# Inverse roots of memory between the forget exits, a warm-up tile written by VectorE, and the weight column on ScalarE's queue

## The reference

```python
def rmsnorm(x, w):
    xf = x.astype(jnp.float32)
    y = xf * lax.rsqrt(jnp.mean(xf * xf, axis=-1, keepdims=True) + EPS)
    return (y * w.astype(jnp.float32)).astype(x.dtype)

def token_mix(h, w_in, ...):
    proj = h @ w_in
    (hq, hf, hi, hgate, gq, gk_, gv, ggate, glr) = jnp.split(proj, idx, axis=-1)
    f = lb + (1.0 - lb) * jax.nn.sigmoid(hf)
    ...
    gdecay = jax.nn.log_sigmoid(glr @ gla_w_gk2 + gla_b_gk) / GLA_GATE_NORMALIZER
    ...

def reference(x, mem, norm_mix_w, w_in, ...):
    h = rmsnorm(x, norm_mix_w)
    x = x + token_mix(h, w_in, ...)
    x = x + cross_attend(rmsnorm(x, norm_xa_w), rmsnorm(mem, norm_mem_w), w_xq, w_xkv, w_xo)
    x = x + moe(rmsnorm(x, norm_moe_w), w_router, b_router, w_gate_up, b_gate_up, w_down, b_down)
    return rmsnorm(x, norm_final_w)
```

## Time and profile before

| | |
|---|---|
| median of three runs | 1184.41 us |
| profiled execution, whole | 1184.76 us |
| span of the profiled execution | 1183.0 us |
| TensorE busy | 1134.4 us (96%) |
| VectorE busy | 381.3 us (32%) |
| ScalarE busy | 181.8 us (15%) |
| read from memory | 442.55 MB |

### The profile page before, as it was taken

One profiled execution on the slowest core, in us unless ns is written; L12 is line 12 of the kernel. 1 busy time (PEld: TensorE's weight loads), 2 busy tenths in 40 slices (PEclk: granted clock), 3 DMA queues, 4 the chain that ended last, 5 costly groups with the idle time before them and its releaser, 6 DMA issues.

```text
span 1183.0 us, 18703 instructions
## 1 busy us (share of the span) xinstructions
PE 1134.4 (96%) x7502; PEld 574.9 (49%) x7503; DVE 381.3 (32%) x891; ACT 181.8 (15%) x395; POOL 22.0 (2%) x65
## 2 busy tenths in 40 slices
PE   9999999999999999999999999999999999999996
PEld 8989889855434444344333333333333333333332
DVE  4988878455221111222211111111111111111112
ACT  4611521343100000000000000000000000000002
POOL 4000010000000000000000000000000000000000
PEclk9999999999999999999999999999999999999999
DMA  9954204989999999999999999999999999999995
GB/s 324 369 172 144 73 10 155 346 330 398 417 428 432 429 431 431 429 433 431 433 430 433 431 430 433 431 431 433 431 433 430 432 432 431 432 432 423 426 424 226
DMA packets 41353, 444.24 MB, mean 376 GB/s; under 512 B 4270, under 2 KB 5656, under 8 KB 24540
## 3 DMA queue, kind: packets, MB, share of 16 engines
q1 hardware_dynamic: 39868, 440.45, 88.9%
q0 software_dynamic: 480, 1.85, 0.6%
q10 hardware_dynamic: 960, 1.31, 0.4%
HBM read 442.55 MB, written 1.05 MB: 375 GB/s over the span
## 4 chain that ended last, share of the span: by engine, by line
PE 67%; DMA 31%; DVE 1%; ACT 0%; SPq 0%; issue 0%; DVEq 0%; ACTq 0%
DMA ring<-in_w_gate_up 30%; PE bank L1180 23%; PE bank L1171 13%; PE bank L736 7%; PE bank L732 4%; PE bank L1210 4%; PE bank L1225 3%; PE bank L875 1%; PE bank L715 1%; PE bank L1107 1%; PE bank L1296 1%; PE bank L1201 1%; PE bank L1287 1%; PE bank L913 1%; PE bank L1019 1%; PE bank L1141 1%
## 5 line engine op out<-in xcount | busy, mean ns | idle before, releaser
L1180 PE MATMUL bank<-ring,region 128*64 128x512 f32 x2048 | 464.0, 608 | 36.0 <-DMA ring<-in_w_gate_up 36.0
L1180 PEld LDWEIGHTS bank<-ring,region 128*64 128x64 f32 x2048 | 147.0, 140 | 333.5 <-issue 268.7
L1171 PE MATMUL bank<-ring,region 128*64 128x512 f32 x1024 | 226.8, 595 | 0.3 <-ACT region L1419 0.3
L2328 DVE TENSOR_SCALAR region<-bank 128x512 f32<-128x512 f32 x32 | 22.1, 691 | 573.9 <-PE bank L1180 573.9
L1171 PEld LDWEIGHTS bank<-ring,region 128*64 128x64 f32 x1024 | 71.1, 137 | 130.1 <-issue 127.2
L1419 ACT ACTIVATE region<-bank 128x256 f32<-128x256 f32 (+1 forms) x130 | 53.4, 437 | 367.0 <-PE bank L1171 251.1
L1419 ACT ACTIVATE bank<-region 128x512 f32<-128x512 f32 x32 | 19.2, 601 | 452.5 <-DVE region L2328 452.5
L736 PE MATMUL bank<-ring 128*128 128x256 f32 x392 | 86.6, 380 | 0.0
L736 PEld LDWEIGHTS bank<-ring 128*128 128x128 f32 x392 | 73.8, 190 | 10.9 <-issue 0.7
L1210 PE MATMUL bank<-region 64*128 64x512 f32 x264 | 65.6, 615 | 0.1
L1225 PEld LDWEIGHTS bank<-region,r_levels 128*128 128x128 bf16 x1536 | 61.3, 118 | 1.6 <-issue 1.6
(11 more groups left out here) (318 smaller groups left out, 774.0 us busy)
## 6 DMA issues: line engine op xcount, KB each, us to landing
ring<-in_w_gate_up SPq DMA_DIRECT2D x48, 4096.0 KB, 30.2
ring<-in_w_down SPq DMA_DIRECT2D x24, 4096.0 KB, 36.5
ring<-in_w_gate_up SPq DMA_DIRECT2D x26, 2048.0 KB, 14.3
ring<-in_w_down SPq DMA_DIRECT2D x10, 2048.0 KB, 13.3
ring<-in_w_in SPq DMA_DIRECT2D x6, 2048.0 KB, 19.8
ring<-in_w_gate_up SPq DMA_DIRECT2D x11, 1024.0 KB, 35.6
ring<-in_w_xkv SPq DMA_DIRECT2D x4, 2048.0 KB, 11.0
ring<-in_w_down SPq DMA_DIRECT2D x7, 1024.0 KB, 8.3
```

What stands on the lines that cost most here:

```text
L1171: last = pe.matmul(bk[half * ROWS:(half + 1) * ROWS, :], lhs, w[:, half * 512:(half + 1) * 512], start=start, stop=stop, skip_group_check= ...
L1180: last = pe.matmul(rows, lhs, columns[:, half], start=start, stop=stop, skip_group_check=True)
L2328: v.tensor_scalar(g_t, bank_g[:, :], LIMIT, None, ALU.min).then_inc(sem["g_clamped"], 1)
```

## The change

Five things are done. The weight column w_mix is issued as the first transfer of ScalarE's queue, ahead of the first part of the forget panel, instead of on SyncE's queue between x's two halves. TensorE's warm-up reads a tile `warm` that VectorE fills with ones as its first instruction, seven products instead of six, and TensorE waits for the identity only after them; an eighth product, on the identity, follows flip_x(0). The loops over token halves and over the first two parts of the forget panel change places: the first half goes through parts 0 and 1 with flip_x(1) between them, then the second half. The mem_sum product stands ahead of m = 3 of the last forget products instead of after them. And VectorE computes the inverse roots of memory between scale_forget(0) and scale_forget(1) instead of between keys_of_forget(0) and keys_of_forget(1).

```diff
-WARM_UP = 6
+WARM_UP = 7
+        warm = r_t[:, 0:P]
@@ sync
             load_x(0)
-            sp.dma_start(w_mix, by_row(A["norm_mix_w"][0])).then_inc(sem["w_mix_in"], 16)
             load_x(1)
@@ tensor
+            def keep_busy(tile, n):
+
+                c = (3 - n // 2) * P
+                pe.matmul(banks[6 + n % 2][:, c:c + P], tile, tile, start=True, stop=True)
+
+            pe.wait_ge(sem["warm_ready"], 1)
+            for n in range(WARM_UP):
+                keep_busy(warm, n)
             pe.wait_ge(sem["ident_ready"], 1)
-            for n in range(WARM_UP):
-                c = (3 - n // 2) * P
-                pe.matmul(banks[6 + n % 2][:, c:c + P], ident[:, :], ident[:, :], start=True, stop=True)
...
             flip_x(0)
+            keep_busy(ident[:, :], WARM_UP)
...
-            for i, (k0, k1) in enumerate(zip(FIRST_ROWS[:2], FIRST_ROWS[1:3])):
-                pe.wait_ge(first_in[i], 16)
-                for t in range(NT):
-                    if (t, k0) == (1, 0):
+            for t in range(NT):
+                for i, (k0, k1) in enumerate(zip(FIRST_ROWS[:2], FIRST_ROWS[1:3])):
+                    if (t, i) == (0, 1):
                         flip_x(1)
+                    pe.wait_ge(first_in[i], 16)
                     for m in range(4):
                         ins = forget(k0, k1, t * P, (t + 1) * P, m)
...
             for m in range(4):
+                if m == 3:
+                    pe.wait_ge(sem["mem_squared"], 1)
+                    end(pe.matmul(begin("mem_sum")[:, 0:8], same_row, mem_sums, start=True, stop=True), "mem_sum")
                 ins = forget(*FIRST_ROWS[2:], 0, T, m)
                 if m % 2 == 1:
                     end(ins, f"hf{m // 2}")
-
-            pe.wait_ge(sem["mem_squared"], 1)
-            end(pe.matmul(begin("mem_sum")[:, 0:8], same_row, mem_sums, start=True, stop=True), "mem_sum")
@@ scalar
+            act.dma_start(w_mix, A["norm_mix_w"][0].rearrange("(p k) -> p k", k=KT)).then_inc(sem["w_mix_in"], 16)
             act.dma_start(panel(0)[:, k, :], first_panel[:, k, :]).then_inc(first_in[0], 16)
@@ vector
+            v.memset(warm, 1.0).then_inc(sem["warm_ready"], 1)
             dve.wait_ge(sem["ident_ready"], 1)
...
             scale_rows(0)
             scale_forget(0)
+            wait_full(dve, "mem_sum")
+            taken(v.tensor_scalar(mem_sums, bank_of("mem_sum")[:, 0:8], EPS, None, ALU.add), "mem_sum")
+            wait_taken(dve, "mem_sum")
+            newton_steps(mem_rstd, mem_sums).then_inc(sem["mem_rms"], 1)
             scale_forget(1)
             scale_rows(1)
...
             keys_of_forget(0)
-            wait_full(dve, "mem_sum")
-            taken(v.tensor_scalar(mem_sums, bank_of("mem_sum")[:, 0:8], EPS, None, ALU.add), "mem_sum")
-            wait_taken(dve, "mem_sum")
-            newton_steps(mem_rstd, mem_sums).then_inc(sem["mem_rms"], 1)
             keys_of_forget(1)
```

More of the change, by code:

```diff
@@ L133 @@
 SEMS = """quarter_joined rows_summed first_product seventh_product first_kept seventh_kept t1_ready t2_ready t3_ready t4_ready w_mix_in pads_zeroed glr_ready hT_scaled mem_in vec_in cols_in glr_in router_in moe_row_in final_row_in down_bias_in gu_bias_in
- consts_ready ident_ready masks_ready s_zeroed x_squared x_diag mem_squared mem_rms mem_scaled mem_turned mem_weighed hf_streamed lb_diff lb_sigmoid lnf_ready
+ consts_ready warm_ready ident_ready masks_ready s_zeroed x_squared x_diag mem_squared mem_rms mem_scaled mem_turned mem_weighed hf_streamed lb_diff lb_sigmoid lnf_ready
  z_abs z_ln scanned first_sigmoids r_diff r_exp r_ready gate_sigmoid gate_ready y_ready x1_squared
```

## The result

| | before | after |
|---|---|---|
| median of 19 runs each, us | 1184.41 | 1186.03 |
| lowest to highest, us | 1183.77 to 1186.52 | 1184.10 to 1189.64 |
| profiled execution, span | 1184.76, 1183.0 | 1186.46, 1184.7 |

The ratio after to before is 1.0015 with a 95% interval of 1.0008 to 1.0022. I had forecast 1183.9 in a range of 1183.0 to 1185.0: "within 0.2%" held, but the sign and the range didn't. The two profiled executions differ by 1.70 us, as the medians do (1.62), so they can be read against each other.

The account below looks back on a forecast made before the run. TensorE's progress up to about 270 us was taken to release the expert weight stream that sets the end. Terms 0 + 0 + 0 - 0.49 gave -0.5 us, so 1183.9 us (chance 0.60), range 1183.0 to 1185.0.

Parts of the forecast that it names:

- within 0.2%: Whole kernel's time: no change beyond 0.2%, which means 2.4 us; chance 0.93, against faster 0.04 and slower 0.03.
- The frame: Whole kernel: a microsecond won on TensorE up to 270 us moves the expert weight stream and the end one for one.
- The query panel as a floor: Queries' start: panel lands at 23.68, so TensorE's earlier savings are spent waiting; products start at 23.70 as now, gain 0.
- Warm-up and forget order: Ahead of the query panel: earlier warm-up gains 0 to 1.5 us, token-half order saves 0.3; both taken as 0.
- Memory's roots: VectorE between the forget exits: moving the inverse roots removes the gap among the gs products, -0.49 us.
- The wait for z: VectorE after the roots' move: next limited by z, ending at 32.94; L1895 starts about 33.05, so 0.57 survives.
- The weight column: Front loads: column lands some 0.4 earlier, VectorE starts at 5.45; forget products at worst 0.45 late; taken as 0.
- The bound of 1.5 us for the displacement: Forget panel's first part: changing places with x's second half, it lands between 5.6 and 7.1; 0.5 MB takes 1.5 us.
- rival c: At 23.7 to 27.1 TensorE idles for the query panel, its clock falls to 1.2 GHz: 1.2 late, 1185.6; chance 0.05.
- The scatter: Whole kernel's time: runs scatter by 0.3 us about their median, allowed for in the range.

Follow-up runs that it names:

- the second experiment: Kernel before with only the weight column's move from SyncE's queue to the head of ScalarE's: 1187.39 us, ratio 1.0021.
- the seventh: Changed kernel with the forget panel's first part on SyncE's queue between x's halves, plus the query panel loaded in two halves: 1183.84 us, ratio 0.9989.
- the sixth experiment: Changed kernel with the forget panel's first part on SyncE's queue between x's halves, the column alone on ScalarE's: 1184.45 us, ratio 0.9993.
- the tenth: Kernel before with only the warm-up on VectorE's tile, seven products and an eighth behind the first transposes: 1185.17 us, ratio 1.0002.
- the first: Changed kernel with the weight column back on SyncE's queue between x's halves: 1184.22 us, ratio 0.9996.
- the eighth: Changed kernel with the column back on SyncE's queue, and ScalarE waiting for the warm-up tile before issuing the forget panel's first part: 1183.94 us, ratio 0.9988.
- the ninth experiment: Kernel before with only the forget products reordered token half by token half: 1184.42 us, ratio 1.0001.
- the third experiment: Kernel before with only memory's inverse roots between the two forget exits and the mem_sum product ahead of m = 3: 1184.41 us, ratio 0.9996.
- fourth experiment: Changed kernel with seven products on the identity instead of one behind the first transposes, keeping TensorE busy: 1184.78 us, ratio 1.0000.

## Why the prediction was wrong, point by point

- **The frame** was right: what TensorE loses by the gs products (1.67) is what the span loses (1.7). Over the other runs it holds less exactly: in the second experiment 2.96 at the end of the gs products became 2.6 of the span, in the seventh a gain of 1.80 became 1.5, in the sixth 1.15 became 0.4, and the tenth was 0.29 earlier there and 0.9 longer in the end. What comes between isn't shown.
- **The query panel as a floor** was right as a wait, and its time is not fixed. TensorE waits for it in the first, sixth, eighth, ninth and tenth experiments, and splitting it lets TensorE through. It hides a loss only as far as TensorE would have been early, and here the loss was larger.
- **Warm-up and forget order**: the start was forecast at 1.05 and found at 1.13. The values of 0 held in the times of their own runs, but their working was short of one thing: what they win ahead of the panel shortens VectorE's queue too and so takes part of the same 0.49 us that the roots' move takes (0.22 and none left in their traces). The gains don't add up.
- **Memory's roots**: -0.49 is the gap that is gone in every kernel that has this part. The wait for z, forecast as the next limit, is there: 0.72 us of VectorE before the z bias in the changed kernel, and 0.73 in the third experiment.
- **The weight column** is the step that failed, in two terms. First, "the products start at worst at 7.1 instead of 6.67, 0.45 late": they started at 8.39. I let the two half megabytes change places in a file served one after another. In the trace the panel's part started behind the column, then shared the engines with x's second half, which had the double share, and after it with the panel's second part. The bound of 1.5 us for the displacement measured 2.7. Two stretches of the trace before could have told me. In 3.0 to 3.5 us of the trace before, both queues are at work and share 69.1% to 28.4%. In 4.0 to 4.5 us ScalarE's has 104.2%, so the part's short landing time rested on having the engines to itself. The gain didn't come either: VectorE was to start weighing at 5.45 and started at 6.01, because x's first half had landed at 4.81 instead of 4.41 and VectorE waited for its transposes, not for the column.
- Second, **the clock**. I had weighed a fall of the clock only at the query panel (rival c), with a price of 1.7. It fell at 9.01, after TensorE had idled 1.86 us for the displaced part, and its price was 1.65. The price was right and the place was wrong: the idle time that the displacement makes was not carried over into that rival, because I had it at 0.45. I had also compared with a row where 1.85 us of idle time did no harm; here 1.86 us did, and 2.14 in the second experiment, while 0.6 in the tenth did not. One such row is no safe side.
- Together: 0.92 + 1.65 late at the queries, 0.9 back up to the gs products' end, +1.67. With the late landing but no fall of the clock the sum is about 0 (fourth experiment, 1.0000).
- **The scatter** of 0.3 in the range came from three executions. Nineteen of the kernel before spread over 2.8.

**What stays open.** The changed kernel scatters over 5.5 us and the kernel before over 2.8. Of the 19 runs of the changed kernel, those at 1188.2 and above have a mean granted clock of 0.982 or 0.983 and those below 1185.9 of 0.985 to 0.987. That fits a fall of the clock whose extent differs from execution to execution, but only one execution of each kernel has a trace, so it isn't shown. Such long executions are not the change's own, either: of 110 executions of the kernel before, those beside the experiments included, 7 took 1187.98 to 1189.00, with a clock of 0.982 to 0.984, against 6 of 19 of the changed kernel at 1188.2 and above. Nor is it shown why the clock rose late in the profiled execution of the third experiment.

## What to carry to other kernels

A transfer moved to the head of another queue is not priced by its own bytes: ask which transfers on the other queues now come abreast of what it pushed back, and what share of the engines each queue then gets. When the first operands of TensorE come later, price the idle time twice, once for the delay and once for the clock that may fall behind it; spare time further on covers only the first part of the sum. And a gain that sits ahead of a transfer landing just in time is spent waiting for it until that transfer is split or brought forward, unless it also shortens another engine's queue, as in the ninth experiment.

## What the runs showed of the hardware

- Two queues with work at the same time passed about as many packets each, 32 and 33 in 5.0 to 5.5 us of the changed kernel, so that packets of 4 KB against 2 KB had 66.5% against 35.8% of the engines' time. A transfer of 4 KB took 5.99 us when it stood behind half a megabyte on its queue, beside another on the other queue.
- TensorE, having reached 2.4 GHz, idled 1.86 us and was set to 1.2 GHz 0.62 us after it had begun to work again, for 3.41 us; in the second experiment, after 2.14 us of idling, 0.56 us after. With seven small products in that time it didn't happen.
- The landing of one and the same panel differs between the traces by 1.5 us, though the same bytes are loaded ahead of it: the query panel landed at 23.12 in the sixth experiment, 23.68 before and 24.58 in the eighth. Part of it is SyncE's issue, at 11.88, 11.88 and 12.48; from issue to landing it took 11.24, 11.8 and 12.10 us.
